# A decoder step in true float32 halves: the attention loop written out, a new order around the two norms, and the cache copies issued from ScalarE

## What is computed

```python
# layer 0: gated convolution module
a, gl, z = split(x @ w_in, 3)                   # 1024 -> 3*1024
u = a * sigmoid(gl)
c = layer_norm(depthwise_conv31(u) + dw_b)      # causal, width 31
x = layer_norm(ALPHA * x + (silu(c) * silu(z)) @ w_out)
# layer 1: three attention groups (window, dilation) = (128,1), (512,4), (2048,16)
h = x @ w_in                                    # 1024 -> 10*1024: q,k,v of each group, and z
o = merge_by_softmax_sum(attention(q_g, k_g, v_g) for g in groups)    # 16 heads of 64
y = layer_norm(ALPHA * x + (o * silu(z)) @ w_out)
# outputs too: the new caches = old cache rows without the first 8, then the 8 new ones
```

## Time and profile before

| | |
|---|---|
| runs | 1279.2, 1280.03, 1282.17 us; median 1280.03 |
| the profiled execution | 1281.31 us, its span 1279.5 us |
| mean granted PE clock | 0.95 of full |
| PE busy | 1140.3 us, 89% of the span |
| DVE, ACT, POOL busy | 561.1, 424.3, 216.9 us |
| transfers | 372.98 MB, mean 292 GB/s |
| chain that ended last | PE 72%, DVE 9%, DMA 8%, issue 5%, ACT 3% |

### The profile page before, as it was taken

How to read it: one execution, slowest core, us unless ns; L and a number is a source line. 1 busy time by engine, 2 the same in 40 slices (tenths; PEclk the granted TensorE clock), 3 DMA queues, 4 the chain that set the end, 5 groups by cost and what they waited for, 6 DMA issues and landing times.

```text
span 1279.5 us, 27381 instructions
## 1 busy us (share of the span) xinstructions
PE 1140.3 (89%) x11168; PEld 1007.2 (79%) x11168; DVE 561.1 (44%) x1530; ACT 424.3 (33%) x868; POOL 216.9 (17%) x98
## 2 busy tenths in 40 slices
PE   7899999298599997999998699999599999958996
PEld 6688888198598996898887699888499888846656
DVE  3999999878603106034104313400423411254324
ACT  5564456532524223123224022321323322321122
POOL 0000000000232232122222022122122222212200
PEclk9899999699799998999999799999899999979997
DMA  9975569999999899579779578977946977987662
GB/s 299 365 262 194 205 234 322 331 339 372 325 379 376 313 360 358 217 248 375 274 253 380 198 251 304 349 280 288 347 156 257 375 271 289 356 310 276 238 243 91
DMA packets 67683, 372.98 MB, mean 292 GB/s; under 512 B 11632, under 2 KB 14576, under 8 KB 64880
## 3 DMA queue, kind: packets, MB, share of 16 engines
q1 hardware_dynamic: 67568, 371.27, 80.7%
HBM read 353.61 MB, written 192.21 MB: 427 GB/s over the span
## 4 chain that ended last, share of the span: by engine, by line
PE 72%; DVE 9%; DMA 8%; issue 5%; ACT 3%; SPq 3%; POOL 0%; DVEq 0%; ACTq 0%; POOLq 0%
PE pairB L509 11%; PE pairA L509 10%; PE pairB L510 8%; PE pairA L510 8%; DMA ring<-k_tiles 7%; PE pairC L707 4%; PE pairA L519 3%; PE pairB L519 2%; PE pairA L520 2%; PE pairC L551 2%; PE pairB L520 2%; PE pairA L887 2%; PE pairB L887 2%; PE pairD L660 2%; PE pairC L660 1%
## 5 line engine op out<-in xcount | busy, mean ns | idle before, releaser
L1225 POOL TENSOR_TENSOR w_lo<-landing,w_hi 128x1024 fp32r<-128x1024 f32 x86 | 205.2, 2386 | 630.6 <-ACT w_hi L965 630.6
L965 ACT ACTIVATE w_hi<-landing 128x1024 fp32r<-128x1024 f32 x86 | 90.9, 1057 | 420.4 <-PE pairB L510 222.9
L509 PE MATMUL pairA<-act_hi,w_hi 128*128 128x320 f32 x312 | 102.5, 328 | 19.7 <-issue 16.7
L1578 DVE COPY v_nat<-pairA 128x512 f32<-128x512 f32 x12 | 8.3, 692 | 234.6 <-PE pairA L775 234.6
L509 PE MATMUL pairB<-act_hi,w_hi 128*128 128x320 f32 x312 | 100.6, 322 | 0.0
L509 PE MATMUL pairA<-act_lo,w_hi 128*128 128x320 f32 x312 | 98.8, 317 | 0.0
L509 PE MATMUL pairA<-act_hi,w_lo 128*128 128x320 f32 x312 | 98.5, 316 | 0.0
L510 PE MATMUL pairA<-act_hi,w_hi 128*128 128x256 f32 x312 | 88.9, 285 | 9.8 <-issue 9.8
L509 PE MATMUL pairB<-act_hi,w_lo 128*128 128x320 f32 x312 | 97.3, 312 | 0.0
L509 PE MATMUL pairB<-act_lo,w_hi 128*128 128x320 f32 x312 | 97.3, 312 | 0.0
L510 PE MATMUL pairA<-act_lo,w_hi 128*128 128x256 f32 x312 | 88.9, 285 | 0.0
(11 more groups left out here) (395 smaller groups left out, 2827.2 us busy)
## 6 DMA issues: line engine op xcount, KB each, us to landing
kept<-cache SPq DMA_DIRECT2D x64, 2040.0 KB, 18.7
landing<-w_units SPq DMA_DIRECT2D x120, 512.0 KB, 7.4
ring<-k_tiles SPq DMA_DIRECT2D x104, 512.0 KB, 6.1
ring<-v_tiles SPq DMA_DIRECT2D x104, 512.0 KB, 5.7
kept<-cache SPq DMA_DIRECT2D x16, 2016.0 KB, 18.6
kept<-cache SPq DMA_DIRECT2D x8, 960.0 KB, 7.5
kv_new<-kT SPq DMA_DIRECT2D x24, 288.0 KB, 2.3
kv_new<-vT SPq DMA_DIRECT2D x24, 288.0 KB, 4.6
```

Source lines behind the costliest of these rows:

```text
L509: pe.matmul(tok(s, 0, SPLIT), lhs, x[:, k, 0:SPLIT], start=first, stop=last)
L965: act.activation(w_hi[:, m % 2, :], landing[:, m % LAND, :], ACT.Copy).then_inc(hi_done, 1)
L1225: return pool.tensor_tensor(dst, src, hi.bitcast(F32), ALU.subtract)
```

## The change

1. On PE, ACT, DVE, POOL and SP the loop over head groups 1 to 3 is written out by Python (`for hg in range(1, HG)`), as is SP's small loop over output units.
2. The 88 copies leave SP's list and go into ACT's, as ACT's own DMA issues, in numbers given by tables per unit. SP keeps loads and stores.
3. Ring tiles are issued up to five ahead of their use, across group ends; the first five already in the middle of group 0.
4. Around the first norm: PE makes 10 taps of the last chunk and DVE 21; the last square comes before two of the silus; ACT touches a one-column tile to load its table early; `gate_low(k)` follows `gate(k)` in the same turn.
5. Around the second norm: PE takes the sums of the last squares itself; four attention units instead of two are multiplied chunk by chunk (evicted from four PSUM pairs), DVE splitting two more units before the norm; POOL clears its rows only when all four units are done.

```diff
+COPIES = [(g, b, piece) for g, n in ((2, 8), (1, 2), (0, 1)) for piece in range(n) for b in range(NB)]
+COPIES_CONV = (0, 0, 1) + (1,) * 9 + (1, 1, 2) * 3 + (2, 1, 1)
+COPIES_OUT = (2, 1, 2, 1, 2, 1, 2, 1)
+COPIES_FIRST = (1, 1, 1, 0) + (1,) * 13 + (1, 0, 0)
+COPIES_HG = (0, 1, 0, 1, 1, 0, 0, 1, 0, 2, 2, 0, 0, 1, 0, 0, 1, 0, 0, 1)
...
+            def load_tiles(end):
+                first, begun[0] = begun[0], max(begun[0], end)
+                for T in range(first, end):
+                    hg, t = divmod(T, TILES_HG) if T < HG * TILES_HG else (HG - 1, T - (HG - 1) * TILES_HG)
+                    which, tt = divmod(t, TILES)
+                    sp.wait_ge(tile_used, T + 1)
...
                     load_unit(N_IN1 + hg * U_HG + m + LAND, m % LAND)
+                    if not first:
+                        load_tiles((hg - 1) * TILES_HG + STEP_AT[m] + RING)
+                    elif m == U_CH:
+                        load_tiles(RING)
                     if i:
                         store_kv(hg, m - 1)
-                    if not first:
-                        for t in range(STEP_AT[m], STEP_AT[m + 1]):
-                            load_tile(hg - 1, t)
...
-            with sp.Fori(1, HG) as hg:
+            for hg in range(1, HG):
                 load_group(hg, False)
...
-            for m in range(2):
+            for m in range(4):
                 pe.wait_ge(w_split, LAND + N_IN1 + m + 1)
             pe.wait_ge(out_part, KC)
-            for k in range(KC):
-                pe.wait_ge(y_split, k + 1)
-                for m in range(2):
-                    for q in range(3):
-                        mm = product(m, N_IN1 + m, k, q, act_hi, act_lo, m)
-                    if k == KC - 1:
+            pe.wait_ge(out_var, 2)
+            for ks in (*((k,) for k in range(KC - 2)), (KC - 2, KC - 1)):
+                pe.wait_ge(y_split, ks[-1] + 1)
+                for m in range(4):
+                    for k in ks:
+                        for q in range(3):
+                            mm = product(m, N_IN1 + m, k, q, act_hi, act_lo)
+                    if ks[-1] == KC - 1:
                         mm.then_inc(proj_done, 1)
...
-            with pe.Fori(1, HG) as hg:
+            for hg in range(1, HG):
                 group(hg, False)
...
+            def copy_rows(g, b, piece):
+                n = COPY_ROWS[g] * 2 * D
+                src = d[f"cache{g}"][bass.ds(b, 1), (piece * n + NQ * 2 * D):(piece * n + NQ * 2 * D + n)]
+                dst = o[f"kept{g}"][bass.ds(b, 1), piece * n:piece * n + n]
+                act.dma_start(dst.rearrange("a (r m) -> (a r) m", r=COPY_RUNS[g]),
+                             src.rearrange("a (r m) -> (a r) m", r=COPY_RUNS[g])).then_inc(copied, 16)
...
             for k in range(KC):
+                if k == KC - 2:
+                    conv_square(KC - 1)
                 act.activation(zs[:, k, :], zs[:, k, :], ACT.Silu).then_inc(silu_done, 1)
-            conv_square(KC - 1)
...
+            load_table(ACT.Sqrt)
             act.wait_ge(conv_sqsum, KC)
...
             for m in range(4, KC):
                 hi0(N_OUT0 + m)
+                copy_next(COPIES_OUT[m - 4] + COPIES_OUT[m])
...
                         if i >= U_CH - 2:
                             split_hi(N_IN1, hg, U_HG, m + 2)
+                        copy_next((COPIES_FIRST if first else COPIES_HG)[m])
...
-            pool.wait_ge(w_split, LAND + N_IN1 + 2)
+            pool.wait_ge(proj_done, N_IN1 + 4)
             pool.memset(q_row[:, :, :, :, :, :], 0.0).then_inc(rows_cleared, 1)
...
                 gate(k)
                 if k + 2 < KC:
                     conv_scale(k + 2)
+                gate_low(k)
                 if k + 3 < KC:
                     conv_center(k + 3)
-                if k:
-                    gate_low(k - 1)
-            gate_low(KC - 1)
```

More of the change, by code:

```diff
@@ L325, in o_own, with evac_pair @@
             return s_probs[:, bh, 0:2 * P]
+        def evac_pair(first, m):
+            return m if first and m < 4 else m % 2
         def turned_bank(b, h):
@@ L809, in group @@
                         m = ch * U_CH + i
-                        if i >= 2:
+                        if first and m in (4, 5):
+                            pe.wait_ge(qkv_out, m - 3)
+                        elif i >= 2 and not (first and m < 4):
                             pe.wait_ge(qkv_out, hg * U_HG + m - 1)
@@ L815, in group @@
                             pe.wait_ge(s_max, (hg * 2 + ch) * 8 - 2)
-                        if not (first and m < 2):
+                        if not (first and m < 4):
                             unit(N_IN1 + hg * U_HG + m, m % 2, act_hi, act_lo)
@@ L823, in group @@
                                 pe.wait_ge(o_out, 1)
+                            elif first and i == 3:
+                                pe.wait_ge(qkv_out, 4)
                             if first and i == 7:
@@ L958, in _, with copy_next @@
         def _(act):
+            copies = iter(COPIES)
+            def copy_next(count):
+                for _ in range(count):
+                    copy_rows(*next(copies))
+            def copy_rows(g, b, piece):
[4 more added lines that the diff above has]
+                             src.rearrange("a (r m) -> (a r) m", r=COPY_RUNS[g])).then_inc(copied, 16)
             def split_hi(base, it, per, m):
@@ L1062, in _ @@
             act.activation(std[:, :], std[:, :], ACT.Sqrt, bias=vec[:, 0, V_EPS:V_EPS + 1]).then_inc(conv_std, 1)
+            load_table(ACT.Silu)
             act.wait_ge(u_stored, 16 * 2 * KC)
@@ L1088, in _ @@
             hi0(N_IN1 + 1)
-            for m in range(4, KC):
-                out_square(m)
+            out_square(4)
+            out_square(5)
+            hi0(N_IN1 + 2)
+            out_square(6)
+            out_square(7)
+            hi0(N_IN1 + 3)
+            load_table(ACT.Sqrt)
             act.wait_ge(out_sum, 1)
@@ L1131, in group @@
                             exp_rows(hg - 1, 0)
-                        if i < U_CH - 2:
+                        if i < U_CH - 2 and not (first and m < 4):
                             split_hi(N_IN1, hg, U_HG, m + 2)
@@ L1142, in group @@
                         if kept is not None:
-                            act.activation(kept, tok(m % 2, 0, NS), ACT.Silu if kind == "z" else ACT.Copy)
+                            act.activation(kept, tok(evac_pair(first, m), 0, NS), ACT.Silu if kind == "z" else ACT.Copy)
                         if kind == "z":
@@ L1175, in _ @@
             group(0, True)
-            with act.Fori(1, HG) as hg:
+            for hg in range(1, HG):
                 group(hg, False)
@@ L1345, in _ @@
                     lo0(nxt[2] + AHEAD)
[L1346 removed]
+                taps(j, VALUE_TAP, DVE_TAPS if j < KC - 1 else LAST_DVE_TAPS)
                 sample_taps(j)
@@ L1655, in _ @@
             group(0, True)
-            with dve.Fori(1, HG) as hg:
+            for hg in range(1, HG):
                 group(hg, False)
```

177 lines of the change are left out of this document (80 added, 97 removed).

## The result

The changed kernel took **1338.99 us** (median of 4 runs, 1334.35 to 1353.4) against 1279.62 for the kernel before on the same chip: a ratio of **1.048**, 95% interval 1.039 to 1.057. The forecast was 1226 with 0.94 on faster. The profiled execution has a span of 1341.8 us, 62.3 more than before.

The account below looks back on a forecast made before the run. PE was taken to bound the kernel, busy 1140 of 1279.5 us, so only its idle and slow-clock time could go. Terms summed to -54.1 from the profiled 1281.3, giving 1227.2, or 1226 against the median; range 1213 to 1250.

Parts of the forecast that it names:

- Load against copy: Ring tile steps beside copies on a second queue: cost 0, at worst 0.5 us per copy in groups 1 to 3.
- Copies starve the tiles: Rival, ring in groups 1 to 3: urgent tiles wait up to 5.6 us per copy, making the kernel slower; chance 0.05.
- Loop: Head-group loop written out: PE's two stops at the jump back and the slow units behind them go, -30.3 us.
- early tiles: Ring tiles issued early: -10.6 us at group 1's start, -3 in later groups, -5 in the tail.
- Convolution: First copies no longer between two loads, so DVE and then PE wait less in the convolution: -1.5 us.
- first norm: Last convolution chunk and first norm: PE starts the output projection about 3.6 us earlier; term -3.7 us.
- Second norm: Before the attention layer: PE starts near 327.2, then idles 7.2 us for POOL before unit 4; net -1.5 us.
- Copies on ACT: 88 copy issues on ACT, at chunk ends and in the output projection: +1.5 us, between 0 and 7.5.
- Sharing costs some: Rival: copies beside loads cost 0.5 us each in the groups, 1242, to 1255 with ACT's full issue cost; chance 0.14.

Follow-up runs that it names:

- run 3: The changed kernel without the 88 copies (old cache rows stay unwritten): 1224.04 us, ratio 0.955 to the kernel before.
- run 1: The changed kernel with the 88 copies back on SP's queue, the same number behind each unit's load: 1243.75 us, ratio 0.973 to the kernel before.
- run 6: The changed kernel with all 88 copy issues left on ACT, each copying only the first 512 B of each copy row: 1227.31 us.
- run 4: The kernel before with only its loops over head groups written out on all five engines: 1263.47 us, ratio 0.986.
- run 10: The changed kernel with the copies on ACT's queue walked so that each packet is 16 KB: 1286.56 us, ratio 1.003 to the kernel before.
- run 5: The changed kernel with the copies on ACT's queue walked in separated blocks, giving 4 KB packets: 1302.98 us, ratio 1.016 to the kernel before.
- run 2: The changed kernel with each copy cut into more rows of about 4 KB, still lying behind one another: 1342.44 us, ratio 1.049 to the kernel before.
- run 7: The changed kernel with the copies back on SP's queue and walked in 4 KB packets: 1262.90 us, ratio 0.984 to the kernel before.

## Why the prediction was wrong, step by step

**The step that failed is "Load against copy": "cost 0, at worst 0.5 us on each of 33 copies in groups 1 to 3".** The bytes of the copies cost 116.7 us of span (the table above; 112 by the medians). Three things in that step were wrong.

- *The price.* It shared the transfers by bytes: "11 us if at full overlap". The queues share by packets, 2.06 us for 0.20 us in the mean. In the groups the cost is 31.6 / 33 = 0.96 us a copy, twice its worst.
- *The place.* It looked at the ring tiles alone, since they come in 8 us steps. 76.5 of the 116.7 us were lost before the attention layer, where only weight units are loaded, over 38 copies: 2.0 us each. Four landing buffers are a lead of four units at best, 26 us at 6.40 each; that is plenty against a load of 3.8 us (run 3) and too little against 75. The prediction had the hint in its own rows, a load of 61.8 us behind seven copies, and the 12 copies over eight units right ahead of the second norm in the diff.
- *The direction.* It read the move off SP's queue as relief from waiting: "a load need not stand behind them". On one queue the wait of a load is bounded by what was issued ahead of it. On two, every packet of every load waits for a copy packet as long as copies are outstanding, whenever they were begun.

**The rival "Copies starve the tiles"** had the mechanism, turns of queues with rows of 4 KB against rows of 64, and the sign. Its place was wrong as well: it looked at the ring in groups 1 to 3, where a copy cost 0.96 us, under its own break-even of 1.6. With the loss of that place alone the kernel would still have been faster (a span of 1225.1 + 31.6, against 1279.5). What made it slower are the weight units ahead of the attention layer, 2.0 us a copy, which no part of the prediction priced. It was given 0.05 because of "one tile and more of lead, and few copies where four tiles are due". Both are facts of the plan; neither says anything about who is served first. The rival's second half, that ACT's issue blocks, was not the case here (0.65 us at most), though it was with small packets.

**The rule of the Trainium skill that was weighed** (Issuing engines are not separate DMA queues) was the wrong one for this question. That transfers of several issuing engines share the same 16 DMA engines is true in this trace: from 330 to 380 us q10 and q1 together fill 99% of them. But the prediction took from it that the second queue is neutral, and it cost 95 us here (run 1). That a queue of long packets takes nearly all could have been asked from the sizes known beforehand.

**The rest of the sum held**, by run 3 (span 1222.6) and run 6 (1225.1). Predicted -54.1 from 1281.3; run 6's profiled execution took 1226.9, -54.4. Agreement to 0.3 us is partly luck: up to the first ring tile run 6 gained 14.2 us of 17.3, and from there to the prompt's output 40.7 of 38.3.

- *Loop -30.3, early tiles -10.6, -3, -5.* From the first ring tile to the prompt's output 635.5 us before, 595.3 in run 3: -40.2, where -30.3 - 3 - 5 = -38.3 was predicted. First ring tile: 16.3 earlier, 17.3 predicted with the norms' terms. The total is right; run 4 shows that its split is not, since the loop alone gives 17.3 us of span and leaves tile waits of 4.80 and 4.14 that the stops had hidden.
- *Convolution -1.5, first norm -3.7.* PE starts the output projection at 250.21 in run 3, -5.7, and at 251.85 in run 6, -4.1, for -5.2.
- *Second norm -1.5.* The predicted start of 327.2 counts this norm's gain only; with the 5.2 us of the terms ahead of it that is 322.0, and run 3 has 321.54. The new wait for POOL ahead of unit 4 is there, 4.72 us, not 7.2, but the four units took 1.9 us longer than the 28.4 predicted. Unit 4 starts at 356.54 in place of 365.5, -9.0, with all terms up to there at -6.7.
- *Copies on ACT +1.5, bounds 0 to 7.5.* 2.5 by spans, 3.3 by medians. "If ACT's queue issues while the split is still running, the cost is 0": it does. The issue begins at 307.67, 0.02 us behind the start of the split at 307.65. But the next instruction waits for all issues ahead of it: four copies in a row left 1.55 us of "issue" before that split.

Two slips. "Sharing costs some" goes up to 1255, but 1242 and ACT's issues at 7.5 in place of 1.5 make 1248 to 1249; nothing hung on it. And in the text ahead of the prediction, the kernel before begins 20 copies in head group 0, not 17 (16 in the convolution, 8 behind it, 8 in the output projection, 6 before the attention layer, 20, and 10 in each of the groups 1 to 3 make 88); 17 is the changed kernel's number. No term rested on it.

What stays open: whether a turn is always one packet. It is so in the counts from 330 to 380 us (351 to 353) and from 164 to 184 (149 to 149). From 160 to 192 as a whole they differ, 233 to 555: 205 of q1's packets fall in the first 4 us and 201, small ones of the stores among them, in the last 8. They differ in runs 10 and 5 too (661 to 722, 2083 to 1079). Where one of the queues has no work for a while, such counts are to be expected; that it was so there is not shown. Nor does the trace name the DMA engine of a packet, so the turns themselves are not seen, only their sums.

## What to carry to other kernels

Before moving bulk transfers to a queue of their own, compare the packet sizes: queues that both have work share the DMA engines by packets, so the one with 64 KB rows took twelve times the bytes of the one with 4 KB rows here. Bulk that nobody waits for belongs behind the urgent loads in the same queue, where a load waits only for what was issued ahead of it, and at a rate the stretch can carry (here 11 copies of 2 MB a group cost 5 us in three groups, 15 cost 50). And ask which in-order engine has a late load's first consumer in front of other work: here weight units that the norm does not use stopped the norm, for some 11 us beyond their own lateness.

## What was not expected of the hardware

- Two queues with work were served 351 to 353 packets, at 2.06 and 0.20 us each in the mean; loads of 512 KB that take 3.8 us in the middle without copies took up to 75.1.
- Cutting a copy whose rows lie behind one another into 16 or 17 times as many rows left its packets as they were: 4096 in all, as in the changed kernel (run 2).
- With copies in 4 KB packets the DMA engines moved 314 GB/s where they moved 364 with rows of 64 KB, full in both and loads among them (runs 7 and 1); and one issue of a copy held its engine for up to 15.05 us with 4 KB packets (run 5), 6.5 with 16 KB (run 10), 0.65 with 64 KB.
- A DMA issue on ACT, 0.52 us, runs beside ACT's own compute; only the next instruction waits for it.
- A stop of one kind hid a wait of another: with the loop's 13 us stops gone, tile waits of 4.80 and 4.14 us appeared at the same places (run 4).
